# Two feed-forward blocks: the second projection's input sums made ahead and fetched per slot by GpSimd's queue

## What is computed

```
h = rmsnorm(x)                                # 256 x 2048
f = square(relu(h @ w_ff1)) @ w_ff2           # 2048 -> 8192 -> 2048
x = x + rmsnorm(f)                            # first block
h = h + square(relu(m)) @ w_down              # second block, m = rmsnorm(h) @ w_up
```

## Time and profile before

| what | value |
|---|---|
| median of 3 runs | 2221.47 us (2220.31 to 2222.43) |
| span of the profiled execution | 2219.3 us, all at a granted clock of 0.999 |
| its own time | the page gives the span alone; the median of the runs is 2.2 us above it |
| busy: PE / DVE / ACT / POOL | 2195.5 / 1613.8 / 1163.2 / 93.2 us |
| first up, down | the down runs from 785 to 1119 us |
| second up, down | the down runs from 1872 to 2207 us |
| DMA | 402.65 MB, 181 GB/s over the span |

### The profile page before, as it was taken

The page is one execution under the profiler, slowest core; times in us unless marked ns, Lnnn a source line. Parts: engine busy times, 40 slices in busy tenths (PEclk is TensorE's granted clock), DMA queues, the critical chain, the costliest instruction groups (busy, mean ns, idle before and its releaser), DMA issues.

```text
span 2219.3 us, 32872 instructions
## 1 busy us (share of the span) xinstructions
PE 2195.5 (99%) x13128; PEld 1892.6 (85%) x13128; DVE 1613.8 (73%) x2013; ACT 1163.2 (52%) x1682; POOL 93.2 (4%) x66
## 2 busy tenths in 40 slices
PE   8999999999999999999999999999999999999998
PEld 7888988888888888888898988888888888888886
DVE  7878565665454599899886578847454547998997
ACT  6433465543443466566664466646434345665665
POOL 0553000000000000000000000000000000000000
PEclk9999999999999999999999999999999999999999
DMA  8364445555556666667654533455565565666663
GB/s 328 121 153 161 151 134 211 168 190 189 189 188 188 187 194 207 195 205 258 199 166 144 172 115 98 136 196 163 187 189 189 189 189 173 215 201 195 209 202 114
DMA packets 169923, 402.65 MB, mean 181 GB/s; under 512 B 15296, under 2 KB 30912, under 8 KB 165968
## 3 DMA queue, kind: packets, MB, share of 16 engines
q1 hardware_dynamic: 158496, 394.83, 55.3%
q10 hardware_dynamic: 11312, 6.22, 1.2%
HBM read 398.90 MB, written 2.13 MB: 181 GB/s over the span
## 4 chain that ended last, share of the span: by engine, by line
PE 94%; DVE 4%; ACT 1%; issue 1%; DMA 0%; SPq 0%; DVEq 0%; ACTq 0%
PE ps L768 21%; PE ps L773 11%; PE ps L841 7%; PE ps L842 6%; PE ps L843 6%; PE ps L657 5%; PE ps L857 3%; PE ps L856 3%; PE ps L858 3%; PE ps L665 3%; PE ps L666 3%; PE ps L667 3%; PE ps L1075 2%; PE ps L1077 2%; PE ps L1076 2%; PE ps L679 2%
## 5 line engine op out<-in xcount | busy, mean ns | idle before, releaser
L2497 DVE TENSOR_TENSOR w_low<-raw_weights,w_high 128x1024 fp32r<-128x1024 f32 (+1 forms) x403 | 474.3, 1215 | 422.1 <-ACT w_high L1574 418.3
L1574 ACT ACTIVATE w_high<-raw_weights 128x1024 fp32r<-128x1024 f32 (+1 forms) x378 | 377.4, 1046 | 408.0 <-PE ps L773 279.8
L768 PE MATMUL ps<-x_split,w_high 128*128 128x512 f32 x2048 | 494.1, 391 | 1.7 <-DVE x_split L2485 1.7
L768 PEld LDWEIGHTS ps<-x_split,w_high 128*128 128x128 f32 x2048 | 374.6, 188 | 74.2 <-issue 3.0
L773 PEld LDWEIGHTS ps<-x_split,w_low 128*128 128x128 f32 x2048 | 265.8, 191 | 12.1
L773 PE MATMUL ps<-x_split,w_low 128*128 128x256 f32 x2048 | 269.4, 283 | 0.0
L841 PE MATMUL ps<-w_high,x_split 128*128 128x512 f32 x672 | 262.0, 390 | 0.5 <-issue 0.4
L842 PE MATMUL ps<-w_low,x_split 128*128 128x512 f32 x672 | 261.5, 389 | 0.0
L843 PE MATMUL ps<-w_high,x_split 128*128 128x512 f32 x672 | 261.4, 389 | 0.0
L2582 DVE TENSOR_TENSOR w_low<-raw_weights,w_high 128x1024 fp32r<-128x1024 f32 x168 | 197.8, 1219 | 1.7 <-ACT w_high L1689 1.6
L1689 ACT ACTIVATE w_high<-raw_weights 128x1024 fp32r<-128x1024 f32 x168 | 167.6, 1045 | 0.0
(11 more groups left out here) (376 smaller groups left out, 3657.9 us busy)
## 6 DMA issues: line engine op xcount, KB each, us to landing
raw_weights<-in_w_ff SPq DMA_DIRECT2D x128, 1024.0 KB, 5.4
raw_weights<-in_w_up SPq DMA_DIRECT2D x64, 1024.0 KB, 5.2
raw_weights<-in_w_down SPq DMA_DIRECT2D x64, 1024.0 KB, 5.5
raw_weights<-in_w_in SPq DMA_DIRECT2D x62, 1024.0 KB, 5.3
raw_weights<-in_w_out SPq DMA_DIRECT2D x32, 1024.0 KB, 4.9
raw_weights<-in_w_mem_kv SPq DMA_DIRECT2D x7, 1024.0 KB, 14.6
residual<-in_xT SPq DMA_DIRECT2D x2, 2048.0 KB, 13.9
region<-t_table ACTq DMA_DIRECT2D x1, 3072.0 KB, 18.9
```

The costliest lines, as they stand in the source:

```text
L768: nc.tensor.matmul(hidden_ps(g)[:, c], w[:, P * c:P * c + P], xs[:, kt], start=(kt == 0), stop=False, skip_group_check=True)
L1574: nc.scalar.activation(split_slot(wh_t, k)[:, r], ring_slot(n)[:, r], ACT.Copy).then_inc(rounded, 1)
L2497: V.tensor_tensor(split_slot(wl_t, k)[:, r], ring_slot(n)[:, r], split_slot(wh_t, k)[:, r].bitcast(f32), ALU.subtract).then_inc(split_read ...
```

## The change

1. **Made once, in the ups.** Two slots after a hidden group is squared, VectorE makes s1 to s4 for the first pair of that group (`parts_summed`), ScalarE rounds 896 columns (three blocks of the even pair, all four of the odd pair) and the four sums, and a slot later VectorE makes the low parts of both (`parts_lowered`).
2. **Stored.** GpSimd's queue writes a record of 1920 columns (960 KB: rounded sums, their low parts, the low parts of both pairs) to an internal DRAM tensor, one per group, 14 an up.
3. **Loaded per slot.** In the downs GpSimd's queue loads, for each summed slot, four pieces into `sl` and `sh` (256, 64, 192 and 192 KB) and for the plain slot behind it the pair's low part (256 KB). It waits for `quad_used` of the summed slot before ahead of the first two, for its `split_used` ahead of the next two, and for an earlier plain slot ahead of the last. TensorE waits for these transfers directly.
4. **Fewer operations in the downs.** VectorE no longer makes the input sums nor these low parts; ScalarE no longer rounds the input sums.
5. **More summed slots.** Every second slot, 2, 4, ..., 28: fourteen of 32 in each pass.
6. `first_product` and `combine` move one slot later, since the last summed slot is 28.

```diff
-        SUMMED = (2, 5, 7, 10, 12, 15, 17, 20, 22, 25, 27)
+        SUMMED = tuple(range(2, PAIRS - 3, 2))
+        LOADED = tuple(r + 1 for r in SUMMED)
+        OWN = (0, 1, PAIRS - 2, PAIRS - 1)
...
-                    pe.wait_ge(sums_ready, 3 * s + 2)
+                    pe.wait_ge(sums_rounded, 3 * s + 1)
+                    pe.wait_ge(xa_loaded, 32 * (s + 1))
...
+                def highs():
+                    act.wait_ge(hidden_ready, i * 2 + (HIDDEN0[name] + g + 1))
+                    act.wait_ge(parts_free, i * 32 + 16 * (FREE0[name] + g))
+                    nc.scalar.activation(x_high, cut(hid_f, i, 1024 * g + P, 2048, 896), ACT.Copy).then_inc(part_rounded, 1)
+
+                def sum_highs():
+                    act.wait_ge(part_summed, i * 8 + 4 * (RECORD0[name] + g))
+                    nc.scalar.activation(s_high, s_sums, ACT.Copy).then_inc(part_rounded, 1)
...
+                        if not first and j in (2, 6):
+                            hidden_parts(name, j // 4 - 1, i)[0]()
+                        if not first and j in (3, 7):
+                            hidden_parts(name, j // 4 - 1, i)[1]()
...
-                nc.scalar.activation(sh[:, 384:896], sums_b[:, 512:1024], ACT.Copy).then_inc(sums_rounded, 1)
...
-                        if r == PAIRS - 3:
+                        if r == PAIRS - 2:
                             first_product(name, h + 1)
...
+            def hidden_stored(name, free):
+
+                free()
+                pool.dma_start(opened, ones[0:1, 0:16]).then_inc(parts_free, 16)
+                for g in range(RECORDS):
+                    pool.wait_ge(part_lowered, 2 * (RECORD0[name] + g + 1))
+                    pool.dma_start(x_records[RECORD0[name] + g], parts_of[name][4]).then_inc(parts_free, 16)
+                pool.wait_ge(parts_free, 16 * (FREE0[name] + RECORDS + 1))
+
+            def hidden_loaded(name):
+
+                sh, sl = sums_x[name]
+                for h in range(2):
+                    for r in SUMMED:
+                        c = summed_count(h, r)
+                        s, x = SUMMED0[name] + c, x_records[RECORD0[name] + SUMMED.index(r)]
+                        if c:
+                            pool.wait_ge(quad_used, s)
+                        else:
+                            pool.wait_ge(split_used, SPLIT0[name])
+                        pool.dma_start(sl[:, 384:896], x[:, 896:1408]).then_inc(xa_loaded, 16)
+                        pool.dma_start(sh[:, 384:512], x[:, 384:512]).then_inc(xa_loaded, 16)
+                        if c:
+                            pool.wait_ge(split_used, SPLIT0[name] + slot_before(c - 1, SUMMED) + 1)
+                        pool.dma_start(sl[:, 0:384], x[:, 512:896]).then_inc(xb_loaded, 16)
+                        pool.dma_start(sh[:, 0:384], x[:, 0:384]).then_inc(xb_loaded, 16)
+                        a, b = loaded_count(name, h, r + 1), plain_count(h, r + 1)
+                        pool.wait_ge(split_used, SPLIT0[name] + slot_before(b - 2, PLAIN) + 1)
+                        pool.dma_start(pair_x[b % 2][1], x[:, 1408:1920]).then_inc(xl_loaded[a % 2], 16)
...
+                def parts_lowered(g, i):
+                    n = 2 * (RECORD0[name] + g - 1)
+                    dve.wait_ge(part_rounded, i * 4 + (n + 1))
+                    V.tensor_tensor(x_low, cut(hid_f, i, 1024 * g + P, 2048, 896), x_high.bitcast(f32), ALU.subtract).then_inc(part_lowered, 1)
...
-                    V.tensor_tensor(s13, x[:, 0:2], x[:, 2::-2], ALU.subtract).then_inc(sums_made, 1)
...
-                    V.tensor_tensor(sl[:, 0:384], pair_of(r, P, 384), sh[:, 0:384].bitcast(f32), ALU.subtract).then_inc(sums_ready, 1)
...
-                    V.tensor_tensor(sl[:, 384:896], sums_b[:, 512:1024], sh[:, 384:896].bitcast(f32), ALU.subtract).then_inc(sums_ready, 1)
...
-                        if r == PAIRS - 2:
+                        if r == PAIRS - 1:
                             combine(name, h + 1)
```

More of the change, by code:

```diff
@@ L210, in program @@
         sums_x = {n: (t[:, 0:896], t[:, 896:1792]) for n, t in (("ff2_1", mixh_t), ("ff2_2", xres_over))}
-        sums_at = [(rinv, place("sums", 22528, 1024)), (region[:, 16384:17408], region[:, 17408:18432])]
+        sums_at = [(rinv, place("sums", 22528, 512)), (region[:, 16384:17408], region[:, 17408:17920])]
+        parts_of = {n: (t[:, 0:896], t[:, 896:1408], t[:, 1408:1920], t[:, 1920:2816], t[:, 896:2816], f[:, 2816:3328])
+                    for n, t, f in (("ff1_1", mixh_t, mix_t), ("ff1_2", xres_over, xres_t))}
         ytok, sq_out = R(6144, TT, D), R(10240, 4, D // 2)
@@ L275, in program @@
         out_written = sem("out_written")
+        parts_free, part_summed, part_rounded, part_lowered = sem("parts_free"), sem("part_summed"), sem("part_rounded"), sem("part_lowered")
+        xa_loaded, xb_loaded, xl_loaded = sem("xa_loaded"), sem("xb_loaded"), [sem(f"xl{i}_loaded") for i in range(2)]
         block = ctx.enter_context(nc.Block())
@@ L471, in summed_count, with own_count, loaded_count @@
             return len(SUMMED) * h + sum(q < r for q in SUMMED)
+        def own_count(name, h, r):
+            return len(OWN) * (2 * (name == "ff2_2") + h) + sum(q < r for q in OWN)
+        def loaded_count(name, h, r):
+            return 2 * RECORD0[name] + len(LOADED) * h + sum(q < r for q in LOADED)
         def slot_before(count, slots):
@@ L830, in plain @@
                     if banks[0] == 0:
-                        pe.wait_ge(chunk_ready, PLAIN0[name] + n + 1)
+                        if r in OWN:
+                            pe.wait_ge(chunk_ready, own_count(name, h, r) + 1)
+                        else:
+                            a = loaded_count(name, h, r)
+                            pe.wait_ge(chunk_rounded, PLAIN0[name] + n + 1)
+                            pe.wait_ge(xl_loaded[a % 2], 16 * (a // 2 + 1))
                         pe.wait_ge(split_ready, 2 * (k + 1))
@@ L1618, in t5_read @@
             def t5_read(chunks):
-                act.wait_ge(chunk_ready, chunks)
+                act.wait_ge(chunk_ready, own_count("ff2_1", 1, 14))
+                act.wait_ge(chunk_rounded, chunks)
                 act.wait_ge(t5_out, 16)
@@ L1659, in final_out, with hidden_parts @@
                                                scale=gain("final", 4 * c + k)), "final", "out", t, c)
+            def hidden_parts(name, g, i):
+                x_high, s_high, s_sums = (parts_of[name][k] for k in (0, 1, 5))
+                def highs():
[5 more added lines that the diff above has]
+                    nc.scalar.activation(s_high, s_sums, ACT.Copy).then_inc(part_rounded, 1)
+                return highs, sum_highs
             def up(name, norm_name):
@@ L2245, in _ @@
             gather("outn", 0, near_sq, 0)
+            hidden_stored("ff1_1", lambda: pool.wait_ge(dve_done, at("t5_masked")))
+            hidden_loaded("ff2_1")
             pool.wait_ge(act_done, at("mlan", "sq", 0))
@@ L2252, in _ @@
             gather("window", 1, xo, 8)
+            hidden_stored("ff1_2", lambda: pool.wait_ge(act_done, at("residual_row", 1)))
+            hidden_loaded("ff2_2")
         @block.vector
@@ L2544, in squared, with parts_summed @@
                     V.scalar_tensor_tensor(h, h, 0.0, h, ALU.max, ALU.mult).then_inc(hidden_ready, 1)
+                x_high, s_high, s_low, x_low, _, s_sums = parts_of[name]
+                s1, s3, s2, s4 = (s_sums[:, P * a:P * a + P] for a in range(4))
+                def parts_summed(g, i):
+                    x = [cut(hid_f, i, 1024 * g + P * a, 2048, P) for a in range(4)]
+                    n = 4 * (RECORD0[name] + g - 1)
+                    dve.wait_ge(hidden_ready, i * 2 + (HIDDEN0[name] + g + 1))
+                    dve.wait_ge(parts_free, i * 32 + 16 * (FREE0[name] + g))
+                    V.tensor_tensor(s1, x[0], x[2], ALU.subtract).then_inc(part_summed, 1)
+                    V.tensor_tensor(s3, x[1], x[0], ALU.subtract).then_inc(part_summed, 1)
+                    dve.wait_ge(part_summed, i * 8 + (n + 1))
+                    V.tensor_tensor(s2, s1, x[1], ALU.subtract).then_inc(part_summed, 1)
+                    dve.wait_ge(part_summed, i * 8 + (n + 3))
+                    V.tensor_tensor(s4, x[3], s2, ALU.add).then_inc(part_summed, 1)
+                def parts_lowered(g, i):
+                    n = 2 * (RECORD0[name] + g - 1)
+                    dve.wait_ge(part_rounded, i * 4 + (n + 1))
+                    V.tensor_tensor(x_low, cut(hid_f, i, 1024 * g + P, 2048, 896), x_high.bitcast(f32), ALU.subtract).then_inc(part_lowered, 1)
+                    dve.wait_ge(part_rounded, i * 4 + (n + 2))
+                    V.tensor_tensor(s_low, s_sums, s_high.bitcast(f32), ALU.subtract).then_inc(part_lowered, 1)
                 def body(i, first=False):
@@ L2548, in body @@
                         low(name, j, i)
+                        if j in (2, 6) and not first:
```

(3 more changed lines are left out.)

69 lines of the change are left out of this document (34 added, 35 removed).

## The result

The changed kernel takes 2250.57 us (median of 4 runs, 2242.11 to 2253.48) beside 2221.24 us for the kernel before: ratio 1.0125, 95% interval [1.0106, 1.0145]. It is slower by 29 us where 7.5 us less was forecast, and above the range's end of 2236. Its profiled execution spans 2240.3 us (its own time, 2242.11 us, is the fastest of the four), so the traces show 21.0 of the 29 us.

A forecast was written before the change was run, and what follows sets the result against it. TensorE's own matmuls were taken to bound the downs, with VectorE close behind. Matmuls saved, 8.16 us, less 0.3 at the end and 0.4 for the 3 MB read gave 2221.5 - 7.5 = 2214.0 us, range 2211.5 to 2236.

The forecast's parts named there:

- The matmuls removed: Downs: fourteen summed slots a pass instead of eleven, 36 matmuls fewer at 0.2267 us, 8.16 us saved.
- The ups: Ups: the added VectorE and ScalarE work and the stores fit into idle time; priced at nothing.
- VectorE and ScalarE in a down: Downs: VectorE 8.7 us and ScalarE 6.4 us a pair, within TensorE's 10.20; priced at nothing.
- The transfers, GpSimd's issue: GpSimd's queue in the downs: 1.41 us an issue, 7.1 of 10.2 us occupied; priced at nothing.
- The first rival: GpSimd's queue sets the pace at each pair's five loads: 2.33 us an issue, 2289 us; chance 0.20.
- The transfers, the landing: Each summed slot's first two pieces land after 6.1 us, inside their 7.48 us window; priced at nothing.
- The DMA engines: Downs: 302 GB/s needed, 376 to 401 seen elsewhere, so room of 6 to 25%; priced at nothing.
- The second rival: DMA engines fill up in the downs: at 290 GB/s a pair takes 10.62 us, 2236 us; chance 0.07.
- Weights: Downs: a weight slot has about 10 us from issue to need and lands in 5.4; priced at nothing.
- The table's 0.4 us: First down: perhaps 0.4 us lost where the 3 MB read meets the new loads.
- The end: Last pass: with `combine` behind slot 28, VectorE readies slot 31 at 10.0 against 9.7 before; 0.3 us more.
- The sum: Whole kernel: 8.16 - 0.3 - 0.4 = 7.5 us less, 2221.5 to 2214.0 us; chance 0.61.

The follow-up runs named there:

- e13: Changed kernel, all 960 KB a pair, second buffer for every second summed slot's four pieces, fifth piece issued ahead of the next four: 2212.64 us, ratio 0.9962.
- e4: Kernel before with fourteen summed slots a pass alone, no records stored or loaded: 2266.88 us, ratio 1.0203.
- e5: Changed kernel with a second buffer for the four pieces, issued a pair earlier; slots 30 and 31 read pair 29: 2230.54 us, ratio 1.0046.
- e9: e5 with the fifth piece issued ahead of the next slot's four pieces: 2215.87 us, ratio 0.9976.
- e1: Changed kernel with all five loads of a pair cut to 16 columns, 40 KB a pair: 2214.12 us, ratio 0.9967.
- e10: e3's 704 KB a pair, with a second buffer for the last three products' pieces: 2225.2 us, ratio 1.0022.
- e15: Changed kernel with the 3 MB table read in the first down cut to one of 16 heads: 2244.31 us, ratio 1.0103.
- e14: Changed kernel, single buffers, with the fifth piece issued ahead of the four: 2261.97 us, ratio 1.0183.
- e3: Changed kernel without the fifth load, VectorE making the plain pair's low part, 704 KB a pair: 2230.89 us, ratio 1.0042.
- e2: Changed kernel with the same five loads issued by ScalarE's queue instead of GpSimd's: 2243.39 us, ratio 1.0096.

## Why the prediction was wrong, point by point

- **The matmuls removed**: right. 36 fewer at 0.2267 us.
- **The ups**: right. Nothing, where it was priced at nothing.
- **VectorE and ScalarE in a down**: right. 8.7 us of a pair were worked out; e13's windows give 163.56 of 189 us, 8.8 a pair, and TensorE doesn't wait for them there. That every second slot can't be summed at no loss without the records is shown by e4.
- **The transfers, GpSimd's issue**: the place was harmless, the size wrong. Taken 1.41 us, with 0.34 and 2.33 as bounds; measured 0.54. The queue is occupied 2.7 us of a pair. The first rival fell. The Trainium skill (SBUF — State Buffer, SBUF: two separate sides) has the rule of the lock that VectorE may hold over GpSimd's descriptors; the trace shows none of it beside two-input subtractions: the 56 issues at `L2319` have a mean of 540 ns, with VectorE busy 83% of the time.
- **The transfers, the landing: this is the step that failed.** The text was "Then the first two land at 2 x 1.41 + 3.3 = 6.1 us, inside 7.48 ... Price nothing". The 3.3 us came from stores of 256 KB in another stage, not from beside a stream of 1 MB loads, and it was taken as the landing of every pair. Measured: the first two have landed 6.6 us after the first's issue at the median, not far from 6.1, but 3.1 to 9.5 us over the slots; 16 of 56 came too late, 14.5 us of stalls. Of the window of 7.48 us some 7.1 are left besides, since the issue follows the release by about 0.4 us. For the next two the prediction gave the window (4.76 to 12.92) and no landing at all: 7.5 us at the median and up to 10.9, 14 times too late for 8.16, 8.3 us and most of another 2.2. e5, e9 and e13, with longer windows at the same bytes, show that it is these two windows.
- **The DMA engines**: the room was there, as argued from the 376 to 401 GB/s: e13 sustains 293 GB/s. But "So there is room ... Price nothing" took rate for delay. Before, the share in the downs was 0.64 to 0.67 and 1 MB landed in 5.4 us; at 0.93 and 0.94 a 64 KB piece takes 5.7 to 6.3. The second rival had the right place and sign, and its 290 GB/s is near what the changed kernel moved (289 and 283). But its mechanism is refuted: the same loads go through in e13 with TensorE never idle in its windows, so a pair takes 10.2 us there and not 10.62.
- **Weights**: "lands in 5.4" became 5.9 and 7.0 (`in_w_down`). The 10 us held: no idle time of ScalarE or VectorE in the downs was ended by a weight load.
- **The table's 0.4 us**: too small. In e1, where little else is loaded, the read already costs 1.6 us, and the stalls of e10 at summed slots (3.6 us) fall within it too. What it costs in the changed kernel is open after e15.
- **The end**: 0.9 us ahead of slot 31 (0.3 before), so 0.6 more against 0.3 forecast.
- **The sum**: with the windows lengthened, e13 takes 8.7 us less than the kernel before (7.5 forecast, 2214.0 against 2212.64). So the other terms of the sum stand; what it missed is the two windows of the pieces, the first with a margin of 1.4 us, the second with none worked out. One slip hangs on nothing: 2221.5 less 8.16 and 1 us is 2212.3, not the 2211.5 at which the range begins.

What stays open: how the loss of a pair is spread. The changed kernel's four runs span 11 us, so which slots stall changes from run to run, and the accounts here are of its fastest one. Why a piece lands after 3 us in one slot and after 9 in the next was read in a few places only (below).

## What to carry to other kernels

Read a landing time from transfers that run beside the stream they will meet, with its spread and not only its median, and compare it with the window from release to need, not the rate with the peak. If the window is short, a second buffer that opens it can be worth more than a smaller load: with single buffers 704 KB gave 2230.9 us, with double ones all 960 KB gave 2230.5 (e5), and 2212.6 once the order fitted as well (e13). Moving a load forward in a queue moves its wait forward too: look at what stands behind it, at the first turn of a loop above all (e14).

## What the runs showed of the hardware

**A small transfer can wait in line behind a large one.** In e3's packet records, two 192 KB pieces (a slot's second set) were issued from 843.86 us on, behind a 1 MB weight load issued at 843.49. Their first packets began at 847.9, when 188 of that load's 256 had begun, and the pieces landed after 5.7 and 7.1 us. ScalarE's queue showed the same in e2: pieces issued from 1013.98 on, behind a weight load issued at 1013.62, had nearly all their packets after 1018 and landed after 6.0 and 7.7 us. The Trainium skill (DMA: Bandwidth & Descriptors, Queues, rings and completion order) says that each engine takes turns between its queues at packet boundaries, and that such a packet is typically 9 to 17 descriptors, which are drained before the switch. A weight load is 256 of the profile's packets, 16 for each engine if they are spread evenly. If these 16 are one packet in the page's sense, a piece waits for all of them, as seen here; if each of them were one, a piece would get its share at once, which these traces don't bear out. No run here tells how they are grouped.

**A stall can halve TensorE's clock.** PE's timeline of the changed kernel, where the first pieces of slot 24 of the last pass came 2.5 us late:

```profile
2181.18 0.39 PE L867 MATMUL ps<-w_high,x_split 128*128 128x512 f32 x1
2183.94 0.47 PE L880 MATMUL ps<-x_split,residual_over 128*128 128x512 f32 x1 [2.37 <-issue]
...
2186.07 0.63 PE L881 MATMUL ps<-x_split,residual_over 128*128 128x512 f32 x1
2186.50 0.63 PE L882 MATMUL ps<-x_split,residual_over 128*128 128x512 f32 x1
...
2188.58 0.39 PE L881 MATMUL ps<-x_split,residual_over 128*128 128x512 f32 x1
```

and its windows (the granted clock is third from the end):

```profile
2183.90:2188.00 4.10, 4.06 (x12) 3.25 (x13) 1.70 (x2) 0.00 (x0) 0.00 (x0) 0.65 0.75 227
2189.00:2193.00 4.00, 4.00 (x19) 3.27 (x19) 2.10 (x1) 4.00 (x6) 2.38 (x5) 1.00 0.88 280
```

From the sixth matmul after the stall on the pitch is 0.43 us instead of 0.227, which is 1.2 in place of 2.4 GHz, seven times in a row: a stall of 2.5 us costs 1.6 us more. Of 14 stalls of 2.0 to 6.6 us in the downs of all runs 11 were followed by such a stretch and three (2.40, 2.42, 2.73) were not; none of the 22 of 1.4 to 1.93 us was.
